# Prompt attention in a hybrid decoder layer: the three sparse branches in steps of a query tile, with the compressed branch taken out of them

## What is computed

```python
# 16 heads in 4 groups of 4; one key and one value head (64 wide) per group
kc, vc = compressed keys and values        # 32 blocks for 512 tokens
s_c = q @ kc.T * scale + bias(dist); p_c = masked_softmax(s_c, dist >= 0); o_c = p_c @ vc
s_s = q @ k_sel.T * scale + bias(dist);    o_s = softmax(s_s) @ v_sel
s_w = q @ k_win.T * scale + bias(dist);    o_w = softmax(s_w) @ v_win
o_A = g0 * o_c + g1 * o_s + g2 * o_w       # sigmoid gates per head and branch
# 8 differential heads (128 wide): two softmax maps each
o_B = rmsnorm((softmax(q1 @ k1.T) - lam * softmax(q2 @ k2.T)) @ v)
h = x + (sig(ga) * o_A + sig(gb) * o_B) @ w_o
```

## Time and profile before

| | us |
|---|---|
| median of 3 runs | 1687.33 |
| lowest and highest run | 1680.70, 1696.27 |
| the profiled execution, its own time | 1688.51 |
| its span, first to last instruction | 1686.7 |
| mean granted TensorE clock, share of full speed | 0.967 |

### The profile page before, as it was taken

How to read it: one execution, slowest core, us unless ns; L and a number is a source line. 1 busy time by engine, 2 the same in 40 slices (tenths; PEclk the granted TensorE clock), 3 DMA queues, 4 the chain that set the end, 5 groups by cost and what they waited for, 6 DMA issues and landing times. The chain is left out here.

```text
span 1686.7 us, 31658 instructions
## 1 busy us (share of the span) xinstructions
PE 1603.4 (95%) x12648; PEld 1327.3 (79%) x12648; DVE 801.3 (48%) x1835; ACT 574.1 (34%) x1197; POOL 173.0 (10%) x269
## 2 busy tenths in 40 slices
PE   8999999998999988899899889999899999999998
PEld 5788888875888875667777676666687999999998
DVE  3776633215443418866666545454364442234322
ACT  5323211323322327756555333233333331123210
POOL 1000000000630000084212000000000000000000
PEclk9999999999999998989989799999999999999999
DMA  6445477434631307454121399999742334333421
GB/s 194 155 158 171 164 257 289 153 91 97 188 106 28 107 10 203 99 184 130 34 89 33 112 391 366 368 345 330 279 151 91 125 100 125 100 125 99 125 75 54
DMA packets 185433, 265.67 MB, mean 158 GB/s; under 512 B 35805, under 2 KB 117149, under 8 KB 185190
## 3 DMA queue, kind: packets, MB, share of 16 engines
q1 hardware_dynamic: 174930, 227.31, 41.3%
q0 software_dynamic: 6016, 25.34, 5.0%
q10 hardware_dynamic: 4372, 11.49, 1.8%
HBM read 241.01 MB, written 42.60 MB: 168 GB/s over the span
## 5 line engine op out<-in xcount | busy, mean ns | idle before, releaser
L641 PE MATMUL pj_ps<-all_hi,pj_xh 128*128 128x512 f32 x480 | 192.6, 401 | 0.0
L643 PE MATMUL pj_ps<-all_hi,pj_xl 128*128 128x512 f32 x480 | 190.6, 397 | 0.0
L642 PE MATMUL pj_ps<-all_lo,pj_xh 128*128 128x512 f32 x480 | 190.5, 397 | 0.0
L1464 ACT ACTIVATE pa_sc<-pa_sc,pa_nmax 128x32 f32<-128x32 f32 (+4 forms) x256 | 125.9, 493 | 112.4 <-DVE pa_nmax L1519 111.9
L2763 PE MATMUL fi_ps<-fi_fl,fi_wh 128*128 128x272 f32 x512 | 148.6, 290 | 0.0
L2764 PE MATMUL fi_ps<-fi_th,fi_wl 128*128 128x272 f32 x512 | 148.3, 290 | 0.0
L2762 PE MATMUL fi_ps<-fi_th,fi_wh 128*128 128x272 f32 x512 | 147.6, 288 | 0.7 <-DVE fi_tl L2541 0.7
L2762 PE MATMUL fi_ps<-fi_fh,fi_wh 128*128 128x272 f32 x512 | 147.8, 289 | 0.0
L2764 PE MATMUL fi_ps<-fi_fh,fi_wl 128*128 128x272 f32 x512 | 147.7, 288 | 0.0
L2763 PE MATMUL fi_ps<-fi_tl,fi_wh 128*128 128x272 f32 x512 | 147.2, 287 | 0.0
L2110 ACT ACTIVATE de_slot<-de_ps_t 128x512 f32<-128x512 f32 (+5 forms) x124 | 62.8, 513 | 172.7 <-PE de_ps_t L1944 84.4
(11 more groups left out here) (347 smaller groups left out, 3164.9 us busy)
## 6 DMA issues: line engine op xcount, KB each, us to landing
de_dv<-in_cache_diff SPq DMA_DIRECT2D x64, 512.0 KB, 9.8
all_big<-in_w_in SPq DMA_DIRECT2D x14, 2048.0 KB, 10.6
de_dk<-in_cache_diff SPq DMA_DIRECT2D x48, 512.0 KB, 9.0
all_big<-in_cache_nsa SPq DMA_DIRECT2D x64, 256.0 KB, 6.5
all_big<-in_w_up SPq DMA_DIRECT2D x16, 1024.0 KB, 5.5
all_big<-in_w_down SPq DMA_DIRECT2D x16, 1024.0 KB, 5.7
all_win<-in_cache_win SPq DMA_DIRECT2D x32, 256.0 KB, 7.7
all_dk<-in_cache_diff SPq DMA_DIRECT2D x16, 512.0 KB, 8.5
```

Of the source, the lines that this page charges most:

```text
L641: pe.matmul(ps[:, t, :], xh[:, k, xk], wh[:, u, k, :], start=k == 0, stop=False)
L642: pe.matmul(ps[:, t, :], xh[:, k, xk], wl[:, u, k, :], start=False, stop=False)
L643: return pe.matmul(ps[:, t, :], xl[:, k, xk], wh[:, u, k, :], start=False, stop=k == KT - 1)
L1464: nc.scalar.activation(tile, tile, ACT.Exp, scale=-1.0, bias=nmax[:, x.n % 6, a:a + 1], accum_out=x.sums[a]).then_inc(probs, 1)
```

## The change

It touches the passages between stages and the sparse half of `prompt_attention`.

Passages. The semaphores `rows_stored`, `cmp_stored` and `oa_out` now live as long as the kernel, and the waits for a stage's last stores move into the next stage: `rows_stored` to SP of `compress` before its first store (and to ACT at v = 2), `cmp_stored` to SP at the start of `prompt_attention` (and to DVE at its first `combine_head`), `oa_out` to SP of `decode_attention` behind its first loads. In `compress`, `lay_out(1)` moves behind the first `low_parts(0)`.

Units. A group has 16 units, selected and window of each pair and tile, so a step of two units is one query tile of one pair. Turned probabilities are now the moving operand: `wide_values` multiplies a block of values (128 keys x 64) as stationary operand with both maps' turned probabilities at once (256 columns); the selected branch goes to PSUM partitions 0 to 63, the window to 64 to 127, alternating. The result stands head-width by queries, so ACT copies it to `o_t` (`wide_copy`) and PE turns it back (`turn_back`, 2 transposes a tile). All four turns of a step now follow each other; `wide_values` of the tile before stands ahead of them and `turn_back` behind.

Compressed branch. Once a group: 16 score matmuls of 32 columns (`cs`), bias added by DVE, one row maximum and one subtraction for all 16 rows of 32 (`cmp_most`), one exponential of 128x512 on ACT, sums and factors (`cmp_sums`), 4 transposes (`cp`), a copy on ACT, 4 matmuls of 256 columns against a block-diagonal value block (`co`), and two DVE products into `cmp_o`. `combine_branches` takes the four products of a tile, adds two and two, and adds `cmp_o`. Its buffers are lent by `win`, so the loads of `win` move: six pages behind the last group's `co`, two into `decode_attention` ahead of its key pages.

Fills and loads. The fills of a group are spread over five steps ahead of it and all are copied by ACT; in group steps ACT takes them ahead of its exponentials. `load_group` is split: 7 loads (q and keys) once the group's buffers are turned, 8 loads (values, bias strip, gates, value blocks) once the group is combined.

```diff
-        NH, NG = DHEADS * QT, 2 * QT * 3
+        NH, NG = DHEADS * QT, 2 * QT * 2
...
-            FILL[b - 4] = [("q", x, 0), ("k", x, 0)]
-            FILL[b - 2] = [("k", x, 1), ("c", x, 0)]
-            FILL[b + 2] = [("q", x, 1)]
+            for n, more in ((-10, [("q", x, 0)]), (-8, [("k", x, 0)]), (-6, [("k", x, 1), ("c", x, 0)]), (-4, [("q", x, 1)]),
+                            (-2, [("cs", x, 0), ("cs", x, 1)]), (4, [("cp", x, 0)]), (6, [("co", x, 0), ("co", x, 1)])):
+                FILL[b + n] = FILL.get(b + n, []) + more
+        MAX_CMP, EXP_CMP, SUM_CMP = ({first_of(g) + n: g for g in range(GROUPS)} for n in (0, 2, 4))
...
+            def wide_values(x):
+                pe.wait_ge(combined, x.tile - 1)
...
+                for k in range(x.t + 1):
+                    for unit in (UNITS[x.n - 1], x):
+                        ins = pe.matmul(unit.wide_part, unit.values[k], p_t[:, unit.br, :, P * k:P * (k + 1)],
+                                        start=k == 0, stop=k == x.t)
+                ins.then_inc(wide_done, 1)
+
+            def turn_back(x):
+                pe.wait_ge(wide_copied, x.m + 1)
+                stand()
+                for a in range(2):
+                    ins = pe.transpose(x.wide[:, a, :], o_t[:, a, :], ident[:])
+                ins.then_inc(valued, 1)
...
+                if NH <= j - LAG - 2 < N:
+                    wide_values(UNITS[j - LAG - 1])
                 for n in (j - LAG, j - LAG + 1):
                     if 0 <= n < N:
                         turn(UNITS[n])
                     for v in VALUES_AFTER.get(n, []):
                         values(UNITS[v])
+                if NH <= j - LAG - 2 < N:
+                    turn_back(UNITS[j - LAG - 1])
...
+                    for x in fills:
                         fill_copy(x)
+                    if j < N:
+                        exps(UNITS[j])
+                    if NH <= j - LAG - 2:
+                        wide_copy(UNITS[j - LAG - 1])
+                    if j in EXP_CMP:
+                        act.wait_ge(cmp_ready, EXP_CMP[j] + 1)
+                        nc.scalar.activation(cmp_p, cmp_p, ACT.Exp).then_inc(cmp_probs, 1)
+                    for n in (j - LAG, j - LAG + 1):
+                        if n < N:
+                            copy(UNITS[n])
+                    if j < N:
+                        exps(UNITS[j + 1])
...
             def combine_branches(x):
-                dve.wait_ge(valued, x.n + 1)
+                dve.wait_ge(valued, NH + x.m + 1)
...
+                step(nc.vector.tensor_tensor(part[:, :, 0, :], part[:, :, 0, :], part[:, :, 1, :], ALU.add))
+                nc.vector.tensor_tensor(oa[:, x.u, x.t, P * x.hp:P * (x.hp + 1)].rearrange("p (h e) -> p h e", h=2),
+                                        part[:, :, 0, :], cmp_o[:, QT - 1 - x.t, 2 * x.hp:2 * x.hp + 2, :],
+                                        ALU.add).then_inc(combined, 1)
```

More of the change, by code:

```diff
@@ L416, in _ @@
             sp.wait_ge(bias_out, 16 * 3)
-            for k in range(3):
-                sp.wait_ge(stored[k], stores[k])
+            shared.rows_level = stores
         @block.scalar
@@ L878, in _ @@
                     act.wait_ge(pe_ready, 1)
+                    for k in range(3):
+                        act.wait_ge(shared.rows_stored[k], shared.rows_level[k])
                 if v % 2 == 0 and v:
@@ L977, in _ @@
                 if v == 0:
+                    lay_out(1)
                     split()
@@ L1174, in prompt_attention @@
         g_in = [s.sem(f"g_in{u}") for u in range(2)]
+        v_in = [s.sem(f"v_in{u}") for u in range(2)]
         h_in = shared.h_in
@@ L1237, in __init__ @@
-                self.clamp = 3e38 if br else 1e29
+                    self.needs += [("k", DHEADS + g, 0), ("k", DHEADS + g, 1)]
+                first, at = P * (QT - 1 - t), 2 * (1 - g % 2)
+                v = (vs, vw)[br]
+                self.lhs = [q_place(g, hp)[x, P * t:P * (t + 1)] for x in HALF]
+                self.width = P * (t + 1)
+                self.rhs = [keys[x, at + br, 0:self.width] for x in HALF]
+                self.values = [v[:, self.u, k, :] for k in range(t + 1)]
@@ L1238, in __init__ @@
+                self.bias = [strip[:, self.u, 2 * hp + x, first:SEQ] for x in range(2)]
+                self.clamp = 3e38
                 self.sums = [rsum[:, self.m % 8, x, br:br + 1] for x in range(2)]
                 self.turns = [("p", n, x) for x in range(2)]
-                self.p_t = [p_t[:, n % 2, x, :] for x in range(2)]
-                self.out = [ps_o[:, self.tile % 2, DK * (3 * x + br):DK * (3 * x + br + 1)] for x in range(2)]
-                self.free_level = n - 1
+                self.p_t = [p_t[:, br, x, :] for x in range(2)]
@@ new lines, in cmp_sums @@
+            def cmp_sums(g):
+                dve.wait_ge(cmp_probs, g + 1)
+                step(nc.vector.tensor_reduce(cmp_coef[:], cmp_p.rearrange("p (n c) -> p n c", c=CHP), AX.X, ALU.add))
+                step(nc.vector.tensor_scalar(cmp_coef[:], cmp_coef[:], TINY, None, ALU.max))
+                step(nc.vector.reciprocal(cmp_coef[:], cmp_coef[:]))
+                for r in range(QT):
+                    mine = cmp_coef[:, HPG * r:HPG * (r + 1)]
+                    step(nc.vector.tensor_tensor(mine, mine, gates[:, g % 2, QT - 1 - r, 0:3 * HPG:3], ALU.mult))
@@ L1848, in _ @@
             load_new(0)
+            for n in range(6, 8):
+                win_page(sp, d, shared, 0, *divmod(n, WINDOW // P))
             for k in range(KEYS_AHEAD, KEY_PAGES):
@@ L1851, in _ @@
             load_new_v(0)
+            for u in range(2):
+                sp.wait_ge(shared.oa_out[u], 32 * (GROUPS // 2))
             for i in range(PAIRS - 1):
```

278 lines of the change are left out of this document (199 added, 79 removed).

## The result

The changed kernel takes 1669.33 us (median of 4 runs, 1663.6 to 1670.31) beside 1687.97 for the kernel before: ratio 0.9873, 95% interval 0.9837 to 0.9908. So it is faster, by 16 to 19 us or about 1%, where the forecast of 1646 promised 41.5. The time lies inside the stated range of 1622 to 1680 but outside the forecast's own 1630 to 1662; it is the one that rival (b) gave, 1670. The profiled execution took 1670.31 us, its span is 1668.4.

A forecast was written before the change was run, and what follows sets the result against it. PE was taken to bound the kernel and its groups. Savings of 36 us in the groups and 4.7 + 2.3 in passages, less 1.5 lost, gave 41.5: 1647, or 1646 at the median; forecast 1630 to 1662, stated range 1622 to 1680.

The forecast's parts named there:

- rival (b): In the groups, PE waits at the third and fourth turn of each step: 24 us, total 1670; chance 0.15.
- The work taken from PE: In the four sparse groups, PE's busy time falls from 225.8 to 188 us.
- Rival (a): Wide value products in the groups do not overlap: groups 252 us, total 1688, no change; chance 0.10.
- The pairs: 80 pairs of 256-column value products in the groups, priced at 0.53 us a pair, 42.4 us.
- the turning back: 64 transposes in the groups at 0.12 us each, 7.7 us, added to PE's work.
- The drain: TensorE drains when its tiling mode switches in the groups: about 3 us over 32 steps, not added to the forecast.
- The passages: Between stages, moved store waits save 4.7 us; in compression, exchanging low parts and rearrangement saves 2.3.
- The gaps: PE's idle time in the groups goes from 20.2 to 22 us, with ends at 14 and 54.
- The ring: Chain of combining, score, exponentials, copies and turns in a group step: 4.3 us a mean tile against PE's 5.9.
- The clock: PE's clock over the groups: 0.91 of full, 18% of the time at 1.2 GHz, kept in the forecast.
- Rival (d): PE at 1.2 GHz for most of the groups: slower from a share of 0.51, total 1743 at 0.8; chance 0.04.
- The loads and the heads: Moved and split loads lose 0.5 us; the last heads, taking over first-group work, lose 1 us.

The follow-up runs named there:

- E9: E6 with ACT's exponentials of a step's first unit behind the first copy of turns instead of behind both; 1645.3 us, ratio 0.9748.
- E1: The kernel before with the passages alone changed: store waits behind the barriers, second rearrangement behind the low parts; 1703.9 us, ratio 0.9951.
- E2: The changed kernel with ACT's wide copy and two copies of turns ahead of its exponentials in a group step; 1679.7 us, ratio 0.9817.
- E5: The changed kernel itself, measured again on a second chip; 1667.7 us, ratio 0.9913.
- E8: E6 with DVE's copy of a step's first turn ahead of the second unit's maximum; 1653.5 us, ratio 0.9825.
- E6: The changed kernel with the edits of E2 and E4 together; 1649.2 us, ratio 0.9786.
- E4: The changed kernel with compressed score matmuls alternating between the two row halves, each half into its own bank; 1685.7 us, ratio 0.9845.
- E12: E6 with the next group's first query half turned ahead of the compressed outputs, and the edit of E11; 1649.4 us, ratio 0.9773.
- E7: The changed kernel with DVE's copy of a step's first turn ahead of the second unit's maximum; 1673.3 us, ratio 0.9934.
- E3: The changed kernel with the second unit's scores between the turns on PE, and DVE's first copy ahead of its second maximum; 1703.5 us, ratio 0.9955.
- E11: E6 with decoding's two window pages asked for behind the key pages; 1648.6 us, ratio 0.9768.

## Why the prediction was right and wrong

**Direction: right**, and the time is within the stated range, though 23 us over the forecast. The main reason is right too: PE bounds the groups, and less work on PE makes the kernel faster.

**The work taken from PE: right.** The forecast was 171 us at full clock, 188 at a low share of 18%. The window says 196.17 at a clock of 0.87, a low share of 26%; by the forecast's own formula 171/(1 - 0.13) = 196.6. Rival (a) is out: wide pairs do run side by side. The profile has 0.53 us for a pair, and 0.50 for one product of the same width alone (the 16 compressed outputs, 8.0 us). E9 is the place to check single prices, since its clock is 0.99 and the sums can be read without a correction. In its groups the 80 wide pairs, and then the turning back:

```profile
710.80:902.40 191.60, 42.48 (x320) 21.75 (x320) 0.99 0.33 103
```

```profile
710.80:902.40 191.60, 12.30 (x64) 7.60 (x64) 0.99 0.33 103
```

The pairs cost 42.5 us (42.4 forecast), the turning back 12.3 (7.7 forecast, 4.6 too low: 0.12 us is the price of a transpose in a long row, and here two stand by themselves, 0.38 us a tile). In the changed kernel at its own clock the compressed scores cost 12.9 (14.7), their transposes 3.4 (1.8), the outputs 8.0 (8.5). The under-priced terms are small and partly offset by the scores. The drain of which the Trainium skill speaks (TensorEngine Tiling (Array Packing), Tiling Modes, Key Properties), 3 us by the forecast's estimate, shows in no row of the changed kernel as a gap of its own. Whether a part of the 4.6 us above is such a drain, inside PE's busy time, these rows cannot tell.

**DVE: right** (160 forecast, 163.5), and **ACT: right** (127.5 forecast, 125.9).

**The passages: right** (7 forecast; 6.8 in the profile, of which 5.1 by the start of attention and 1.7 behind the groups; none of the waits of the earlier trace rows is left; the first wide product, forecast without a wait, still waits 0.97 us; 9.1 measured by E1 with 3.8 to 12.8).

**The gaps: wrong, the step that failed.** "Before, the gaps were 20.2 us; I put 22": they are 34.8. The ring was named in the prediction, with the copy "behind the exponentials of the new tile", and its length weighed as a mean, 4.3 us against PE's 5.9. What decides is not the mean. In the steps of the compressed maximum DVE has 1.8 us more to do ahead of its scores, a term that the ring of the mean tile does not hold; the exponential comes up to 3.7 us later and takes the copy behind it along. These steps and the other gaps of 1 us or more make up 14.3 of 24.4 us. E2 shows the cause of the longest ones: with the copies moved ahead of the exponentials and nothing else changed, PE's wait for ACT's copy falls from 19.6 to 7.4 us, and the gaps by 6.4. That is half of the 12.8 us by which the gaps exceeded the forecast. The rest is spread over waits that the prediction did not price either: 6.7 us until DVE has read the compressed outputs, 3.2 for DVE's copies, 1.9 ahead of the last values of the heads. Rival (b), which had 0.15, had the mechanism and the place. That its time of 1670 came out as well is in part luck: it put 24 us into the gaps, which came out 12.8 above the forecast, and the clock made up most of the difference.

**The clock: in the profiled execution the second part of the shortfall.** The forecast kept 0.91. 196.2 - 188 = 8.2 us of the shortfall are PE's work at a lower clock, and 34.8 - 22 = 12.8 are the gaps: together the 21 us by which the groups missed 210. Rival (d) had a share of 0.26 at 1.2 GHz instead of over 0.51. But the heads went the other way in the same execution, from 0.91 to 0.97, and over the whole span the clock is 0.967 before and 0.965 after. How much the clock weighs is seen within one kernel. Taking 2 x (1 - clock) x span as the time at 1.2 GHz, two executions of E5, of 1678.16 and 1662.67 us, have clocks of 0.961 and 0.973, so 131 and 90 us of it: 15.5 us of time for 41. Over 104 executions (the changed kernel, E1 to E8 and the kernel before beside them), each against the mean of its kernel and chip, 1 us more at 1.2 GHz goes with 0.33 us more time. By medians the changed kernel has 106 such us in E5, the kernel before 101 beside it, and E6 79. So 9 of the 18.5 us between the changed kernel and E6 go with the clock, and the rest with gaps and compressed scores; between the kernel before and the changed one it is under 2 us.

What lowers the clock is only in part shown. Long gaps are one candidate, by the windows around 817 us. The order of the runs does not bear it out by itself: E4 has 42.8 us of gaps, and waits of up to 3.3 us for ACT's copy, at a clock of 0.95, where the changed kernel has 35.1 at 0.86. The compressed scores that keep to one row half are the other. Against the kernel before on the same chip, the median time at 1.2 GHz is 14 us less in E4, 22 in E6 and in E8, and 46, 39, 36 and 29 in E9 to E12, which all have the paired scores. Without them it is 9 less in E2 and 5 and 13 more in E5 and E7; E3 has 1 more. So the pairing probably gave more than its 5 us of work, through the clock, and the order of ACT's queue may have given some of it too; no run takes the two apart beyond this. A test of the gaps alone, with other work in the pause, was not made.

**The loads and the heads: small, as forecast.** The heads take 1.5 us more (1 forecast). Decoding took 316.8 us instead of 314.4 in the two profiles (0.5 forecast), but such differences come and go between executions, as E11 and E12 show, so nothing is put down to it.

**The better version.** E6 and E9 beat both kernels: 34.6 and 44.5 us under the kernel before on their chips, with one line of ACT's order and one loop of compressed scores changed. By ratio that is 1652 and 1645 us where the kernel before takes 1688, close to the 1646 that were forecast for the changed kernel. A second set of turned tiles, with which the wide values could stand between the turns, was not tried.

## What to carry to other kernels

When an instruction of an engine's queue releases a buffer for the engine that bounds the kernel, put it ahead of every instruction that waits for a third engine: a copy of 0.6 us cost 3 us because it stood behind an exponential that could not start. Weigh such a ring at its worst steps and not at its mean, since slack in one step pays for no delay in another; put into the ring what each helping engine does only now and then. And look at the granted clock window by window: here half clock followed long gaps of TensorE, but also narrow products on one row half with no gap at all, and with those paired there was less of it.

## What the runs showed of the hardware

- Two products of 256 float32 columns on the two column halves of the array, with all 128 rows in use, run side by side: 80 pairs in 42.5 us at a clock of 0.99, 0.53 a pair, against 0.50 for such a product alone.
- 64 products of 32 columns take 12.9 us when each bank's products keep to one row half, and 7.5 us when the halves alternate into two banks. PE's busy share does not show the difference, as PE is busy throughout in both (3.23 of 3.23 and 1.87 of 1.87 us a group); only the sum for the line does. Behind the first kind half clock followed in 14 of 20 cases, behind the second in 8 of 28.
- 1 us more at 1.2 GHz goes with 0.33 us more time in this kernel, over 104 executions.
- On the chip of E1 to E4 the compression stage is some 25 us longer in every profile (245.1, 244.3, 243.7 and 245.1 us, against 218 to 220 on the others), and the kernel before is 23 to 29 us slower there. The loss lies in one place: PE stands still 0.8 to 2.9 us again and again from 434 to 457 us, with nothing that the profile shows to wait for ("issue"), and most of that stretch runs at 1.2 GHz. Three such rows of E1, and its window:

```profile
438.36 0.59 PE L1063 MATMUL cm_ph<-cm_xh,all_hi 128*128 128x512 f32 x1 [2.08 <-issue]
...
448.21 0.58 PE L1065 MATMUL cm_ph<-cm_xh,all_lo 128*128 128x512 f32 x1 [2.91 <-issue]
...
453.17 0.59 PE L1064 MATMUL cm_ph<-cm_xl,all_hi 128*128 128x512 f32 x1 [2.24 <-issue]
```

```profile
435.00:470.00 35.00, 19.45 (x68) 13.31 (x68) 6.09 (x9) 7.19 (x10) 13.87 (x15) 0.66 0.42 122
```

What causes it stays open. It is why ratios, and not times, are compared across chips here.
